# Ones products in TensorE's waits, a row-major norm order and spread-out rope sums in a fused two-block kernel

## What is computed

```python
for l in range(2):
    x = x + 0.5 * swiglu(rms_norm(x, ffn1_norm[l]), ...)          # d_ff 2816
    p = rms_norm(x, mix_norm[l]) @ w_in[l]
    attn = mla_group(p[..., :384], p[..., 384:640], p[..., 640:672], ...)  # 8 heads, q and k of 64+32
    conv = conv_group(p[..., 672:], ...)                          # 31 taps per channel, layer norm, silu
    x = x + concatenate([attn, conv]) @ w_out[l]
    x = x + 0.5 * swiglu(rms_norm(x, ffn2_norm[l]), ...)
    x = rms_norm(x, post_norm[l])
```

## Time and profile before

| | |
|---|---|
| time, median of 3 runs | 2367.66 us |
| the profiled execution: its time, its span | 2379.02 us, 2377.4 us |
| TensorE busy | 2282.8 us (96%) |
| VectorE busy, ScalarE busy | 1705.9 us (72%), 1106.4 us (47%) |
| mean granted TensorE clock | 0.970 |
| chain that ended last | PE 77%, DVE 14%, ACT 5%, issue 2%, DMA 1% |
| moved by DMA | 298.65 MB, mean 126 GB/s |

### The profile page before, as it was taken

How to read it: one execution, slowest core, us unless ns; L and a number is a source line. 1 busy time by engine, 2 the same in 40 slices (tenths; PEclk the granted TensorE clock), 3 DMA queues, 4 the chain that set the end, 5 groups by cost and what they waited for, 6 DMA issues and landing times.

```text
span 2377.4 us, 37814 instructions
## 1 busy us (share of the span) xinstructions
PE 2282.8 (96%) x13746; PEld 1988.6 (84%) x13746; DVE 1705.9 (72%) x3268; ACT 1106.4 (47%) x1768; POOL 99.5 (4%) x155
## 2 busy tenths in 40 slices
PE   7999989998999989998999999999999999999999
PEld 7998778998998868997777778888887888888889
DVE  6877848778877957888545555444445898888996
ACT  4343245345344145345455553333433666666664
POOL 0000000000000000001122110011100000000000
PEclk9999879999999979999999999999999999999999
DMA  7564207554554305554344342222112222222222
GB/s 290 196 228 161 77 29 266 216 200 181 210 222 168 124 10 217 198 210 152 72 80 67 74 97 71 71 71 68 67 61 71 100 87 79 88 88 80 88 97 89
DMA packets 82056, 298.65 MB, mean 126 GB/s; under 512 B 10165, under 2 KB 10677, under 8 KB 81333
## 3 DMA queue, kind: packets, MB, share of 16 engines
q1 hardware_dynamic: 78192, 284.72, 33.5%
q0 software_dynamic: 2048, 4.20, 3.1%
q10 hardware_dynamic: 1736, 8.67, 1.0%
HBM read 296.51 MB, written 1.05 MB: 125 GB/s over the span
## 4 chain that ended last, share of the span: by engine, by line
PE 77%; DVE 14%; ACT 5%; issue 2%; DMA 1%; DVEq 0%; ACTq 0%; SPq 0%
PE ps L728 48%; PE ps L760 11%; PE ps L827 4%; DVE wsplit L2096 3%; PE ps L1317 2%; DVE work L2785 2%; PE ps L1178 1%; DVE work L2797 1%; DMA ring<-panels 1%; ACT wsplit L1445 1%; PE ps L1042 1%; PE ps L1056 1%; ACT work L1452 1%; PE ps L1032 1%; DVE work L2817 1%
## 5 line engine op out<-in xcount | busy, mean ns | idle before, releaser
L728 PE MATMUL ps<-hsplit,wsplit 128*128 128x256 f32 (+1 forms) x8376 | 1392.2, 323 | 22.4 <-DVE wsplit L2096 9.8
L728 PEld LDWEIGHTS ps<-hsplit,wsplit 128*128 128x128 f32 x8376 | 1210.9, 191 | 152.8 <-DVE wsplit L2096 16.6
L2096 DVE TENSOR_TENSOR wsplit<-ring,wsplit 128x1024 fp32r<-128x1024 f32 x465 | 570.2, 1235 | 255.1 <-ACT wsplit L1445 252.7
L1445 ACT ACTIVATE wsplit<-ring 128x1024 fp32r<-128x1024 f32 x465 | 490.9, 1057 | 534.4 <-PE ps L728 395.9
L760 PE MATMUL ps<-wsplit,fsplit 128*128 128x512 f32 x1056 | 256.7, 392 | 1.1 <-DVE wsplit L2096 1.1
L760 PEld LDWEIGHTS ps<-wsplit,fsplit 128*128 128x128 f32 x1056 | 192.7, 188 | 37.8 <-DVE wsplit L2096 1.3
L2148 DVE SCALAR_TENSOR_TENSOR work<-ring,cs,work 128x128 f32<-128x128 f32 x672 | 211.9, 357 | 8.8
L1528 ACT ACTIVATE work<-ps 128x256 f32<-128x256 f32 x88 | 33.8, 384 | 176.4 <-PE ps L728 176.4
L2285 DVE SCALAR_TENSOR_TENSOR work<-work,vec 128x256 f32<-128x256 f32 x240 | 100.9, 479 | 1.7
L728 PEld LDWEIGHTS ps<-wsplit,hsplit 128*128 128x128 f32 x768 | 95.6, 197 | 4.5 <-issue 3.0
L728 PE MATMUL ps<-wsplit,hsplit 128*128 128x256 f32 x768 | 97.1, 289 | 1.1 <-DVE wsplit L2096 1.1
(11 more groups left out here) (371 smaller groups left out, 2347.9 us busy)
## 6 DMA issues: line engine op xcount, KB each, us to landing
ring<-panels SPq DMA_DIRECT2D x539, 512.0 KB, 4.5
work<-latent_weights ACTq DMA_DIRECT2D x2, 2304.0 KB, 14.1
work<-rpb POOLq DMA_DIRECT2D x64, 64.0 KB, 6.6
cst<-constants ACTq DMA_DIRECT2D x1, 1408.0 KB
work<-x SPq DMA_DIRECT2D x1, 1024.0 KB, 5.4
work<-post_rows ACTq DMA_DIRECT2D x2, 512.0 KB, 4.4
cT<-ctx ACTq DMA_DIRECT2D x1, 1024.0 KB, 7.8
out<-xT SPq DMA_DIRECT2D x1, 512.0 KB, 2.7
```

The lines of the kernel that those rows point to most:

```text
L728: ins = mm(out_, w(a), x(b), start=start and n == 0, stop=stop and n == 2, **kw)
L1445: af(wsplit[:, split_slot(name, n), 0, :], ring[:, slot, :], ACT.Copy).then_inc(high_ready, 1)
L2096: tt(parts[:, 1, :], ring[:, slot, :], parts[:, 0, :].bitcast(fp32), ALU.subtract)\
```

## The change

1. **Norms.** The last two down panels of a feed-forward, and the last two `wout` panels of a mixer, are multiplied for rows 0 to 127 first and then for rows 128 to 255. The norm's steps follow the rows: add, square, sum, factor and scale rows 0 to 127, then the same for the others; VectorE scales three of the four half blocks. The high and low parts of the next section's second panel come after the norm instead of in it. The post norm's factor is one Ln and one Exp.
2. **Ones products.** `keep_clock(bank, count)` multiplies the matrix of ones by itself, `count` times, 128 columns wide, into a bank that is free; nobody reads it. It stands in the norms (4, or 16 where q is 3 or 6) and in the mixer (20, 12, 6, 2 and 2).
3. **Rope and latent sums** are issued between the products of panels 8 to 12 and of the first head projection.
4. **Loads.** The ring's sections begin at other slots; the load of a feed-forward's last ada panel goes after the next section's first loads. At the start x comes in two loads, the ring's loads no longer wait for the small constants, and the large constants and the latent weights are loaded later.

```diff
+SLOT_OF = {"ffn1": 0, "win": 1, "wout": 0, "ffn2": 1, "A": 5, "B": 5, "OAB": 4, "C": 6, "OC": 6}
...
-        return ((1 if self.name in ("A", "B") else 0) + p % self.slots) % SLOTS
+    def slot(self, p, l=0):
+
+        return (SLOT_OF[self.name] + (3 * l if self.name in SLOT_LAYER else 0) + p % self.slots) % SLOTS
...
-            sp.dma_start(xg[:, :, :], x_in).then_inc(rows_loaded, 16)
+            for t in range(2):
+                sp.dma_start(xg[:, t:t + 1, :], x_in[:, t:t + 1, :]).then_inc((x_ctx_loaded, rows_loaded)[t], 16)
...
+            def keep_clock(bank, count):
+
+                for _ in range(count):
+                    mm(ps[:, bank, 0:128], ones[:, :], ones[:, :], start=True, stop=True)
+
             def turn(q, banks):
 
-                for half in range(2):
-                    for t in range(2):
-                        pe.wait_ge(*((row_stage, 4 * q + 3 + half) if t == 0 else (rstd_ready, 3 * q + 2 + half)))
+                if q > 0:
+                    if q == 3 * LAYERS:
+                        pe.wait_ge(ctx_rstd, 1)
+                    keep_clock(7, 16 if q % 3 == 0 else 4)
+                    pe.wait_ge(x_ready, (q - 1) // 3 * 16 + (4, 8, 16)[(q - 1) % 3])
+                for t in range(2):
+                    for half in range(2):
...
+                r = FT // 2 - 2
+                with pe.Fori(0, r) as i:
+                    six(i)
...
+                six(r, (0,))
+                ada_sum(l, f, ADA_PER_FFN - 2)
+                down(3 * FT - 1, 1, fb + FT, tiles=(0,))
+                down(10, 0, r * 2 + fb + 3, r, tiles=(1,))
+                down(3 * FT - 1, 1, fb + FT, tiles=(1,))
...
+                win(8, 1, 0, between=lambda j: rope(j))
+                win(9, 1, 1, between=lambda j: rope(4 + j))
+                win(10, 3, 0, between=lambda j: rope(8 + j))
+                win(11, 3, 1, between=lambda j: rope(12 + j))
+                pe.wait_ge(lat_ready, l * 2 + 1)
+                win(12, 4, 0, between=lambda j: latent_sum(j // 2, 0, j % 2))
                 pe.wait_ge(lat_ready, l * 2 + 2)
...
+                            if t == 0:
+                                last = latent_sum(n, 1, k)
...
+                pe.wait_ge(v_ready, l * 2 + 2)
+                keep_clock(1, 20)
                 pe.wait_ge(conv_sq_ready, l + 1)
                 for c in range(4):
                     last = mm(ps[:, 0, 0:T], ones[:, :], conv_sq[:, c, :], start=c == 0, stop=c == 3)
                 last.then_inc(conv_var_done, 1)
+                keep_clock(1, 12)
                 turn_heads(0)
                 turn_heads(1)
...
                 for h in range(HEADS):
+                    if h < 3:
+                        keep_clock(1, 6 if h == 0 else 2)
                     transposes(h)
...
-                for n in range(3, KD):
+                for n in range(3, KD - 2):
                     wout(n)
+                for t in range(2):
+                    for n in range(KD - 2, KD):
+                        wout(n, (t,))
...
+            def row_norm(l, u):
+
+                q, src = l * 3 + u + 1, xg if u == 2 else xN
+                sq0 = l * 15 + 4 + 4 * u
+                if u == 1:
+                    low("ffn2", l, 0)
+                row_block(l, u, 0)
+                row_block(l, u, 1)
...
+                else:
+                    row_sums(0, sq0 + 2)
+                    row_block(l, u, 2)
+                    row_block(l, u, 3)
+                    row_scaled(q, 0, 0, src)
+                    row_scaled(q, 0, 1, src)
+                    row_sums(1, sq0 + 4)
+                row_scaled(q, 1, 0, src)
+                if u == 2 and l + 1 < LAYERS:
+                    low("ffn1", l + 1, 0)
...
             def turned(q, gain, banks, name, l):
...
+                low(name, l, 1)
+                if l > 0 and q == 3 * l:
+                    ada_last(l - 1, 1, range(0, 4))
                 low(name, l, 2)
...
+                if (l, f) == (0, 0):
+                    act.dma_start(cst[:, 128:NCONST], consts_in[:, 128:NCONST]).then_inc(const_loaded, 16)
...
+                    act.dma_start(lat[:, :].unsqueeze(1), lat_in[0:1].rearrange("a p m -> p a m")).then_inc(lat_loaded, 16)
...
-            dve.wait_ge(const_loaded, 48)
             dve.wait_ge(constants_set, 1)
...
+            first_high("A")
+            low("A", 0, 0)
...
+            ctx_scaled(range(3, KD))
```

347 lines of the change are left out of this document (181 added, 166 removed).

## The result

| | before | after |
|---|---|---|
| time, median of 6 runs each | 2371.36 us (2367.12 to 2372.45) | 2355.89 us (2353.96 to 2358.85) |
| ratio, 95% interval | | 0.9942 (0.9932 to 0.9953) |
| the profiled execution: time, span | 2379.02, 2377.4 us | 2353.96, 2352.3 us |
| its granted clock | 0.970 | 0.991 |

The change makes the kernel 15.5 us faster, by 0.6%. The forecast was 2340.5, 27.2 us less than before; the measured time is 15.4 above it and just inside the range's upper end.

A forecast was written before the change was run, and what follows sets the result against it. TensorE is busy 2282.8 of 2377.4 us, so only its waits and half-clock stretches can yield time. Mixers 19, norms 4.7 and start 3.5 make 27.2, off the median 2367.66: 2340.5 us, range 2326 to 2357.

The forecast's parts named there:

- I sum against it and take the sum off the median: Gains sized on the profiled execution of 2379.02 us, 11.4 above the median, then subtracted from the median of 2367.66.
- Mixer: 4.5 + 4.0 + 1.0 = 9.5 us, 19 for two: Each mixer: first probabilities 4.5 us earlier, attention's four heads 4.0 less, first wout panel 1.0 less.
- the ring: Loads: other slots, late ada panel and leaner tail of the load order were to cost nothing.
- norms before ffn2: Norm before each second feed-forward: 1.3 us less, from 2.3 earlier less 0.9 for the low part; twice 2.6.
- start: Kernel's start: load queue's wait for small constants goes, most late-panel waits go; 3.5 us less (2 to 5).
- norms before the mixers: Norm before each mixer: half the turns done early, 1.0 us less, 0.5 with the clock an even chance; twice 1.0.
- between the layers: Norm between the layers: 3.2 us saved, less 1.6 for VectorE's low parts and ada steps; net 1.6.
- before section A: Norm before section A: gain in the wait handed back by panel 2's low part; -0.5 us (-1.5 to +1).
- The 0.7 taken off for the twelve: Mixer: 12 ones products behind the sum of squares take 2.6 us, partly on the path; 0.7 us of cost.
- Rival 1: Attention: the clock falls there all the same; 14 us gained instead of 27.2, so 2353; chance 0.3.
- Rival 2: Mixers: thin rope passes hide under wide ones, 2.8 us more saved a mixer, so 2335; chance 0.08.
- Rival 3: Mixers: ones products at half clock delay due work, 12 us lost a mixer, so 2384; chance 0.03.

The follow-up runs named there:

- experiment 11: Changed kernel without ones products, rope in a block, start's constants as before, ring offset 1: 2372.65 us (first); also panel 6 loaded behind 7 and 8: 2370.52 us (second).
- experiment 8: Changed kernel with ring offset 1 a layer, not 3: 2352.90 us; also panel 6 behind 7 and 8: 2350.44; that without the norms' ones products: 2349.96.
- 9: Changed kernel with the start's constants waited for and loaded as before, x still in two loads: 2364.08 us, ratio 0.9968 to before.
- experiment 3: Changed kernel without any of its 132 ones products: 2366.09 us, ratio 0.9973 to before.
- 7: Changed kernel with rope and latent sums back in a block behind panel 12: 2362.65 us, ratio 0.9964 to before.
- experiment 6: Without the 12 ones products behind the sum of squares, on experiment 8's version without the norms' ones products: 2353.14 us against 2349.96.
- experiment 4: Changed kernel without the 48 ones products in the norms, the mixers' 84 kept: 2355.79 us, ratio 0.9936 to before.
- experiment 5: Only the 20 ones products kept in each mixer, on experiment 8's version without the norms' ones products: 2357.05 us against 2349.96.

## Why the prediction was wrong

**The step that failed first** is in the opening part: "I sum against it and take the sum off the median." With it the largest term, "Mixer: 4.5 + 4.0 + 1.0 = 9.5 us, 19 for two", was sized on an execution with some 40 us at half clock around each mixer. Against that trace it is right (19.6). Against a kernel without the ones products and the spread rope whose profiled execution is at its own median (experiment 11, first, some 30 us at half clock) the same two parts are worth 13.8, in the other such trace 11.0. The trace of before has 143 us at half clock, 25 more than the usual execution, and the change leaves 44 in its own. Of the 11.7 us between 27.2 and the measured 15.5, the two traces' distances from their medians are 9.6 (7.7 for before, 1.9 for after). The hint was in the table: 2379.02 beside three runs of 2367 to 2372. I named those 11.4 us and did not ask in which stages they lie; that they lie in the mixers is what experiment 11 suggests, since unprofiled executions of before have no rows to show it. A further 3.7 us of the missed 2340.5 is the median of three runs, which was low.

**The second** is "The ring's other slots, the late ada panel and the leaner tail of the load order cost nothing: from section A on TensorE never waits for a load." The argument covered section A onward; the loss came before it, where the late ada panel, the order of the loads and the rotation meet. It is 5.7 us by the stage's length and 5 to 8 by the runs (experiment 8).

That the sum of 27.2 comes near the 25.1 between the two traces is in part luck: the ring's -5.7, put at nothing, and the norms before ffn2, 1.7 too high, are made good by the start (2.3 more than summed) and the norms before the mixers (2.4 more).

The terms, against the table of leads:

| term | summed | in the traces | by the experiments |
|---|---|---|---|
| start | 3.5 (2 to 5) | 5.8 | 6.1 (9) |
| mixers, two | 19 | 9.9 + 9.7 | 11 to 14 (traces of 11); 12 to 17 (runs of 3 and 7 together) |
| norms before mixers, two | 1.0 | 1.6 + 1.8 | all norms: none measured (11) |
| norms before ffn2, with its panels | 2.6 | 0.6 + 0.3 | |
| between the layers | 1.6 | 1.5 (3.2, less 1.7 in the feed-forward) | |
| before section A | -0.5 | -0.5 | |
| the ring | 0 | -5.7 | -5 to -8 (8) |

Leaving out one part at a time gives, by the ratios to before, 7.3 us for the ones products, 5.2 for the rope, 5.7 for the start and -5.9 for the slots: 12.3, beside 13.3 to 13.8 for the whole change. The parts account for it without the norms.

- *Start:* mis-sized. I let the waits for late panels go in the main and allowed for losses further on, and put an early panel at half clock. All of them went, and nothing came back.
- *Mixers:* the mechanism is right, and against the trace of before so is the size, 9.5 for 9.8: L948 starts 4.1 us earlier behind the mixer's first product than L904 did (3.7 forecast), the four heads and their ones products take 9.1 us instead of 12.4 (300.43 and 313.40 to the first wout panel; 4.0 less forecast, 3.3 measured), the first wout panel 3.0. The 0.7 taken off for the twelve was no cost (experiment 6); they fill a wait for VectorE. For the usual execution the term is too large, as said above.
- *Norms:* the clock did not fall before a mixer, with the ones products or without (experiment 4), and 8 of 16 turns were done early; 1.7 each, not 0.5. Before ffn2 the waits at the first and second panel (1.06 and 0.51 us, below) took more than I gave. By experiment 11 none of these microseconds is shown in the time.

```profile
345.96 3.47 PE L736 MATMUL ps<-hsplit,wsplit 128*128 128x256 f32 x24 [1.06 <-DVE hsplit L2220]
349.95 2.29 PE L736 MATMUL ps<-hsplit,wsplit 128*128 128x256 f32 x17 [0.51 <-DVE wsplit L2145]
```

- *Rival 1, the clock falls in the attention:* not in this kernel, 3.4 us of half clock a mixer instead of 23.8. It is what happens when the few ones products among the heads (10 in a mixer) are missing: with none (experiment 3) or the 20 alone (experiment 5) four heads run at half clock, and when only the 12 go they don't (experiment 6). The Trainium skill, "TensorE: Matmul & The Clock Gate", Part 4: PE-mode transpose, says that the full clock doesn't engage for transposes. At the start the trace says otherwise: 16 turns, and then 24 passes in 3.31 us, full clock. Between the layers 16 turns ran at full clock behind ones products (1.94 us) and at half behind a wait of 4.07 us (3.65, experiment 4). Experiment 5 is what the rule would give, but waits of 2 to 4 us lie between the turns there, and the runs don't part the two.
- *Rival 2, thin passes are nearly free:* no. Four wide passes with two of the rope's between them take 1.09 us (254.97 - 253.88, with two of the latent sums' alike, 256.06 - 254.97). In the trace of before 87 wide passes without thin ones between them took 18.78 us to the rope's first, 0.216 each, so four are 0.86: 0.11 for a thin one, beside wide products as in the block (0.118). The Trainium skill, "TensorE: Matmul & The Clock Gate", Step-by-step: what each phase is for, has TensorE pull weight loads ahead of products under way; nothing of a thin pair's time was hidden here.
- *Rival 3, the ones products as a cost:* no, 4.73 us in a wait that was 5.0.
- *Slips that leave the sum alone:* the clock row is below 9 in three slices in all, two in the first layer and one in the second, not in three of each. A mixer whose attention stays at half clock comes to 2.8 (4.5 - 4 x 0.43), not 2.9, with the rope nearly free to 12.3, not 12.5; 2.3 less 0.9 is 1.4, not 1.3.
- *Chances:* faster was given 0.94 and came. The range (2326 to 2357) held the time by a microsecond, and by luck: its upper end was set for rival 1, which did not happen. The two errors that mattered, the unusual trace and the ring, were in none of the rivals.

## What to carry to other kernels

- When the profiled execution is far from the median of the runs, find out first in which stages the difference lies. If the change removes just that (here: half clock), its gain must be summed against the usual execution; the granted clock of each run, where it is given, says how far off the trace is (here within 1 us for two of three profiled executions, and 6.5 us short for the third).
- Products whose result nobody reads pay if they stand in every wait of a chain that ends at half clock and keep clear of due work. One gap left open (here that of the six, two and two among the heads) loses most of what the others bring. In a wait that ends with little to multiply behind it (the norms) they bring nothing.
- A load queue that works in order is as late as the slot that comes free last. After every change of slots or of the order of loads, look for the one load whose slot the slowest reader still holds, and for what stands behind it.

## What the hardware showed that was not expected

- Executions of one and the same kernel, the one before, spread over 21 us (2360.34 to 2381.38), and the span follows the granted clock from 0.980 to 0.969, by 0.31 us for each us at half clock. With the clock kept up the changed kernel spreads over 5 us at 0.988 to 0.991.
- All three profiled executions of that kernel are near the top of its spread (2378.2 to 2381.0); those of the changed kernel are at the bottom of its own (2353.96, 2356.35). A comparison of traces alone would have found 25 us for a gain of 13.6 to 15.5, and 11 for the norms' order, for which the runs show none.
- A wait of 3.4 us on TensorE was followed by 24 passes at half clock (5.49 us for 3.1): a late load costs its wait and nearly as much again.
